# FFN of a hybrid diffusion layer: up-projection by one level of Strassen's algorithm, down-projection as a token-major stage of its own

## The reference

```python
D_MODEL = 1024; SEQ = 128; DEC_SEQ = 1024; D_FF = 2816
def rmsnorm(x, gain):
    y = xf * lax.rsqrt(jnp.mean(xf * xf, axis=-1, keepdims=True) + EPS)
    return (y * gain).astype(x.dtype)
def conv_ffn(h, w_up, conv_w, conv_b, w_down):
    u = h @ w_up                                  # (tokens, 2 * D_FF)
    up = jnp.pad(u, ((0, 0), (1, 1), (0, 0)))
    u = up[:, :-2] * conv_w[0] + up[:, 1:-1] * conv_w[1] + up[:, 2:] * conv_w[2] + conv_b
    a, b = jnp.split(u, 2, axis=-1)
    return (jax.nn.silu(a) * b) @ w_down
...
    h = rmsnorm(xs, norm2[l]) * (1.0 + sc2) + sh2
    xs = xs + g2 * conv_ffn(h, w_up[l], conv_w[l], conv_b[l], w_down[l])
y_sample = rmsnorm(xs, final_norm)                # and the same for the context tokens
```

## Time and profile before

| | us |
|---|---|
| median of 3 runs | 2656.23 (2655.0 to 2657.93) |
| profiled execution, its span | 2655.1 |
| PE busy in the span | 2551.0 (96%) |
| PEld busy | 2357.2 (89%) |
| DVE busy | 1698.7 (64%) |
| ACT busy | 1031.5 (39%) |
| POOL busy | 837.8 (32%) |

### The profile page before, as it was taken

How to read it: one execution, slowest core, us unless ns; L and a number is a source line. 1 busy time by engine, 2 the same in 40 slices (tenths; PEclk the granted TensorE clock), 3 DMA queues, 4 the chain that set the end, 5 groups by cost and what they waited for, 6 DMA issues and landing times. The chain is left out here.

```text
span 2655.1 us, 40132 instructions
## 1 busy us (share of the span) xinstructions
PE 2551.0 (96%) x14417; PEld 2357.2 (89%) x14417; DVE 1698.7 (64%) x2807; ACT 1031.5 (39%) x1924; POOL 837.8 (32%) x779
## 2 busy tenths in 40 slices
PE   5999999999998999999999999999999999999997
PEld 3899999999997977788778776798999999999997
DVE  5046556646748368787687677456776677766775
ACT  5223323323323256666666667433122221122114
POOL 1122223223223433433433325633222222322322
PEclk9999999999999999999999999999999999999999
DMA  9611111111110200010010012302111111111111
GB/s 320 202 36 49 37 41 42 44 34 50 44 36 27 63 12 9 25 40 9 25 47 9 2 52 70 114 22 64 42 46 39 40 47 39 39 47 39 39 32 72
DMA packets 164537, 135.92 MB, mean 51 GB/s; under 512 B 18492, under 2 KB 142300, under 8 KB 164444
## 3 DMA queue, kind: packets, MB, share of 16 engines
q1 hardware_dynamic: 163228, 129.99, 15.8%
q10 hardware_dynamic: 1216, 4.72, 0.5%
HBM read 120.41 MB, written 14.29 MB: 51 GB/s over the span
## 5 line engine op out<-in xcount | busy, mean ns | idle before, releaser
L390 PE MATMUL mix_ps<-act_hi,w_hi 128*128 128x384 f32 (+1 forms) x1320 | 443.4, 336 | 6.1 <-ACT conv L2494 3.0
L391 PE MATMUL mix_ps<-act_lo,w_hi 128*128 128x384 f32 (+1 forms) x1320 | 442.4, 335 | 0.0
L392 PE MATMUL mix_ps<-act_hi,w_lo 128*128 128x384 f32 (+1 forms) x1320 | 442.2, 335 | 0.0
L390 PE MATMUL proj_ps<-act_hi,w_hi 128*128 128x384 f32 x1152 | 406.9, 353 | 3.3 <-ACTq L743 3.3
L392 PE MATMUL proj_ps<-act_hi,w_lo 128*128 128x384 f32 x1152 | 387.1, 336 | 0.0
L391 PE MATMUL proj_ps<-act_lo,w_hi 128*128 128x384 f32 x1152 | 387.0, 336 | 0.0
L2604 DVE SCALAR_TENSOR_TENSOR resid_t<-mix_ps,mod,resid_t 128x384 f32<-128x384 f32 (+2 forms) x640 | 273.9, 508 | 134.5 <-PE mix_ps L392 134.5
L1946 DVE TENSOR_TENSOR probs_lo<-mix_ps,probs_hi 128x512 fp32r<-128x512 f32 x324 | 222.7, 688 | 142.5 <-ACT mix_ps L1741 138.9
L1740 ACT ACTIVATE probs_hi<-mix_ps 128x512 fp32r<-128x512 f32 x324 | 193.6, 598 | 183.8 <-PE mix_ps L1540 182.2
L390 PEld LDWEIGHTS mix_ps<-act_hi,w_hi 128*128 128x128 f32 x1320 | 248.4, 188 | 11.6 <-issue 5.4
L2582 DVE SCALAR_TENSOR_TENSOR conv<-up,conv_t,conv 128x127 f32<-128x127 f32 (+1 forms) x168 | 211.4, 1317 | 73.2 <-ACT conv L2510 61.5
(11 more groups left out here) (301 smaller groups left out, 5403.5 us busy)
## 6 DMA issues: line engine op xcount, KB each, us to landing
w_raw<-in_w_in SPq DMA_DIRECT2D x64, 512.0 KB, 3.8
w_raw<-in_w_up SPq DMA_DIRECT2D x44, 512.0 KB, 3.8
ada_w<-in_ada_w SPq DMA_DIRECT2D x7, 2048.0 KB, 15.4
w_raw<-in_w_down SPq DMA_DIRECT2D x22, 512.0 KB, 3.5
q_k_dec<-in_ada_w SPq DMA_DIRECT2D x5, 2048.0 KB, 8.0
out<-xy SPq DMA_DIRECT2D x9, 512.0 KB, 2.7
w_raw<-in_w_o SPq DMA_DIRECT2D x8, 512.0 KB, 5.3
xy<-in_x_sample SPq DMA_DIRECT2D x8, 512.0 KB, 6.7
```

Of the source, the lines that this page charges most:

```text
L390: nc.tensor.matmul(out, w_hi, x_hi, start=(k == 0), stop=False)
L391: nc.tensor.matmul(out, w_hi, x_lo, start=False, stop=False)
L392: return nc.tensor.matmul(out, w_lo, x_hi, start=False, stop=last)
```

## The change

- **Up.** For pairs 1 to 21 the product of a pair is one level of Strassen's algorithm (the form with seven products). The 1024 input features are halved (K1, K2), the tokens are taken in two pieces p of 576, each halved again into 288 (Q, the slices N1 and N2), and the two feature blocks of the pair are the two halves of the output. A piece then takes seven products, each over four k-tiles, 12 matmuls of 288 columns, in place of eight block products. Sums of the activations are made once (`token_sums` in place in `resid_t`, high parts by ACT and low parts by DVE); sums of the weights are made for each pair by POOL (`weights`), whose seven operands are split by ACT (high parts) and POOL (low parts), 512 elements a row each. The results are put together by five DVE additions and two ACT copies a piece (`taken`). Convolution, silu and gate run a piece behind, on 575 or 577 tokens.
- **Gated rows through DRAM.** The gated result goes unsplit to `g_dram`.
- **Down.** A stage of its own after the last pair: 66 steps d = 22 g + f, each with one w_down block (all 22 are read three times) and one 384-token slice of gated rows. Tokens are now the stationary operand and 512 output features the moving one: 18 matmuls of 512 columns a step, added up in six PSUM banks over the 22 pairs of a group. The residual, kept as rows in DRAM (`x1_dram`, 18 stores, made by transposes in stage 1 and 2), is added once per token tile (`residual_rows`), then the final norm.
- `final_norm` and the gates are loaded as rows; the transposes at the end are gone. `normed` works in place in `resid_t`, so `normed_hi` has two ACT instructions where there was one. Phase 2 clears 46 semaphores on POOL at its start.

```diff
+    x1_dram = nc.dram_tensor("resid_scratch", (NT, P, D), F32, kind="Internal").ap()
+    g_dram = nc.dram_tensor("gated_scratch", (FB, P, T), F32, kind="Internal").ap()
...
+        Q = T // 4
+        K1, K2 = slice(0, 4), slice(4, 8)
+        N1 = [slice(2 * Q * p, 2 * Q * p + Q) for p in range(2)]
+        N2 = [slice(2 * Q * p + Q, 2 * Q * p + 2 * Q) for p in range(2)]
+        OUT = [(0, 2 * Q - 1), (2 * Q - 1, T)]
+        SLOT_H = [WH[:, 2, K1], WH[:, 2, K2], WX[:, 0], WH[:, 0, K1], WH[:, 0, K2], WH[:, 1, K1], WH[:, 1, K2]]
+        SLOT_L = [WL[:, 2, K1], WL[:, 2, K2], WX[:, 1], WL[:, 0, K1], WL[:, 0, K2], WL[:, 1, K1], WL[:, 1, K2]]
+        W_SUM = [None, 1, 2, 0, None, None, 1]
+        RAW = [W_RAW[:, 0, K1], None, None, None, W_RAW[:, 0, K2], W_RAW[:, 1, K2], None]
+        SRC = [RAW[i] if W_SUM[i] is None else ST[:, W_SUM[i]] for i in range(7)]
...
# SyncE
+                store_g(0, 0, C_G + 1)
+                load_up(2, 1)
+                with sp.Fori(0, FB - 3) as r:
+                    store_g(r, 1, r * 2 + (C_G + 2))
+                    store_g(r + 1, 0, r * 2 + (C_G + 3))
+                    load_up(r + 3, r + 2)
...
+                store_g(FB - 3, 1, 2 * (FB - 3) + C_G + 2)
+                store_g(FB - 2, 0, 2 * (FB - 3) + C_G + 3)
+                sp.wait_ge(w_ok[5], F)
+                load_wd(0)
+                load_wd(1)
+                store_g(FB - 2, 1, 2 * (FB - 2) + C_G + 2)
+                store_g(FB - 1, 0, 2 * (FB - 2) + C_G + 3)
+                for p in range(2):
+                    sp.wait_ge(g_st[p], 16 * F + 1)
+                sp.wait_ge(w_ok[6], F)
+                for d in range(3):
+                    load_g(d)
+                store_g(FB - 1, 1, 2 * (FB - 1) + C_G + 2)
+                sp.wait_ge(prod, C_P + 14 * F)
+                sp.wait_ge(gate_st, 32)
+                for i in range(3):
...
# GpSimd, in place of split(s, f, n)
-                def split(s, f, n):
-                    pool.wait_ge(raw_in[s], f * 16 + 16)
-                    if s < 2:
-                        pool.wait_ge(up_done, f * 6 + (3 * s - 3 + C_UP))
-                    else:
-                        pool.wait_ge(dn_done, f * ND + 1)
-                    pool.sem_inc(w_go, 1)
-                    nc.gpsimd.tensor_copy(WH[:, s], WR[s]).then_inc(w_hi, 1)
-                    pool.wait_ge(w_hi, n)
-                    nc.gpsimd.tensor_tensor(WL[:, s], WR[s], WH[:, s].bitcast(F32), ALU.subtract).then_inc(w_split[s], 1)
+                def weights(f, sums, his, ahead):
+                    for s in range(2):
+                        pool.wait_ge(raw_in[s], ahead)
+                    nc.gpsimd.tensor_tensor(ST[:, 0], W_RAW[:, 1, K1], W_RAW[:, 1, K2], ALU.add).then_inc(w_sum, 1)
+                    nc.gpsimd.tensor_tensor(ST[:, 2], W_RAW[:, 0, K1], W_RAW[:, 1, K1], ALU.subtract).then_inc(w_sum, 1)
+                    pool.wait_ge(w_sum, sums + 1)
+                    nc.gpsimd.tensor_tensor(ST[:, 1], ST[:, 0], W_RAW[:, 0, K1], ALU.subtract).then_inc(w_sum, 1)
+                    low(0, his + 1)
+                    low(1, his + 2)
+                    pool.wait_ge(w_ok[1], f)
+                    nc.gpsimd.tensor_tensor(ST[:, 1], W_RAW[:, 0, K2], ST[:, 1], ALU.subtract).then_inc(w_sum, 1)
+                    for i in range(2, 7):
+                        low(i, his + i + 1)
...
# TensorE, in place of up_part and down_part
-                def up_part(f):
-                    for s in range(2):
-                        pe.wait_ge(w_split[s], f + 2)
-                        for g in range(NG):
-                            n = NG * s + g
-                            pe.wait_ge(up_out, f * 6 + (n - RING_UP + 1 + C_UO))
-                            for k in range(KC):
-                                m = three_pass(nc, up[:, n % RING_UP, 0:G], WH[:, s, k], WL[:, s, k],
-                                               HH[:, k, g * G:(g + 1) * G], HL[:, k, g * G:(g + 1) * G], k, k == KC - 1)
-                            m.then_inc(up_done, 1)
+                def product(p, i, bank, adds):
+                    hi, lo = sums(p, i)
+                    out = ps[:, bank, 0:Q]
+                    for k in range(4):
+                        nc.tensor.matmul(out, SLOT_H[i][:, k], hi[:, k], start=(k == 0 and not adds), stop=False, skip_group_check=adds)
+                        nc.tensor.matmul(out, SLOT_H[i][:, k], lo[:, k], start=False, stop=False, skip_group_check=adds)
+                        m = nc.tensor.matmul(out, SLOT_L[i][:, k], hi[:, k], start=False, stop=(k == 3), skip_group_check=adds)
+                    m.then_inc(prod, 1)
+                    weight(0)
+                    pe.wait_ge(act_ev, 2 * g + 1)
+                    product(p, 0, p, False)
+                    weight(1)
+                    pe.wait_ge(dve_ev, 5 * g + 2)
+                    if first:
+                        pe.wait_ge(sum_lo[p], 2)
+                    product(p, 1, 2, False)
+                    weight(2)
+                    pe.wait_ge(dve_ev, 5 * g + 3)
+                    product(p, 2, 3, False)
+                    weight(3)
+                    pe.wait_ge(dve_ev, 5 * g + 1)
+                    if first:
+                        pe.wait_ge(sum_lo[p], 4)
+                    product(p, 3, 4 + p, False)
+                    weight(4)
+                    pe.wait_ge(act_ev, 2 * g + (C_A + 1))
+                    product(p, 4, p, True)
+                    weight(5)
+                    pe.wait_ge(dve_ev, 5 * g + 5)
+                    product(p, 5, 6, False)
+                    weight(6)
+                    pe.wait_ge(dve_ev, 5 * g + (C_D + 3))
+                    product(p, 6, 4 + p, True)
+                pe.sem_inc(prod, C_P)
...
+                for d in range(ND):
+                    g, f = divmod(d, FB)
+                    pe.wait_ge(wd_ok, d + 1)
+                    pe.wait_ge(gd_ok, d + 1)
+                    for i in range(3):
+                        n = 3 * g + i
+                        if f == 0:
+                            if g == 0:
+                                pe.wait_ge(act_ev, C_A + 4 * F)
+                                pe.wait_ge(dve_ev, C_D + 10 * F - 5 + (0, 2, 4)[i])
+                            elif n == 3:
+                                pe.wait_ge(dve_ev, C_D + 10 * F)
+                            else:
+                                pe.wait_ge(z_out, 2 * (n - 4) + 2)
+                        for half in range(2):
+                            out = ps[:, SETS[n % 4][half], :]
+                            cols = slice(half * 512, half * 512 + 512)
+                            gh, gl = (GHL[:, d % 3, b, i * P:(i + 1) * P] for b in range(2))
+                            nc.tensor.matmul(out, gh, WDH[d % 3][:, cols], start=(f == 0), stop=False)
+                            nc.tensor.matmul(out, gl, WDH[d % 3][:, cols], start=False, stop=False)
+                            m = nc.tensor.matmul(out, gh, WDL[d % 3][:, cols], start=False, stop=(f == F))
+                        if f == F and i < 2:
+                            m.then_inc(tile_done, 1)
+                    m.then_inc(d_done, 1)
...
# VectorE
+                def token_sums(p):
+                    h11, h12, h21, h22 = X1[:, K1, N1[p]], X1[:, K1, N2[p]], X1[:, K2, N1[p]], X1[:, K2, N2[p]]
+                    dve.wait_ge(lo_ok, 16 + 8 * p)
+                    nc.vector.tensor_tensor(h11, h12, h11, ALU.subtract).then_inc(sum_ok[p], 1)
+                    nc.vector.tensor_tensor(h12, h22, h12, ALU.subtract).then_inc(sum_ok[p], 1)
+                    dve.wait_ge(sum_ok[p], 1)
+                    nc.vector.tensor_tensor(h22, h22, h11, ALU.subtract).then_inc(sum_ok[p], 1)
+                    dve.wait_ge(sum_ok[p], 3)
+                    nc.vector.tensor_tensor(h21, h21, h22, ALU.subtract).then_inc(sum_ok[p], 1)
...
+                def taken(r, p):
+                    g = r * 2 + p
+                    before = r if p == 0 else r + 1
+                    base = r * 12 + 8 if p == 0 else r * 12 + 12
+                    conv(1 - p, before, base, g * 2 + 2)
+                    dve.wait_ge(prod, 7 * g + (C_P + 2))
+                    dve.wait_ge(act_ev, 2 * g + (C_A + 1))
+                    nc.vector.tensor_tensor(TMP[:, 2, :], ps[:, 2, 0:Q], TMP[:, p, :], ALU.add).then_inc(dve_ev, 1)
+                    gate(1 - p, r * 12 + (12 if p == 0 else 20), g + 2, before * 16 + 1)
+                    dve.wait_ge(prod, 7 * g + (C_P + 3))
+                    dve.wait_ge(dve_ev, 5 * g + (C_D + 1))
+                    nc.vector.tensor_tensor(TMP[:, 3, :], ps[:, 3, 0:Q], TMP[:, 2, :], ALU.add).then_inc(dve_ev, 1)
+                    dve.wait_ge(prod, 7 * g + (C_P + 4))
+                    dve.wait_ge(dve_ev, 5 * g + (C_D + 2))
+                    nc.vector.tensor_tensor(U[:, 1, N2[p]], ps[:, 4 + p, 0:Q], TMP[:, 3, :], ALU.add).then_inc(dve_ev, 1)
+                    dve.wait_ge(prod, 7 * g + (C_P + 6))
```

(3 more changed lines are left out.)

782 lines of the change are left out of this document (438 added, 344 removed).

## The result

The changed kernel takes 2694.25 us (median of four runs, 2691.8 to 2696.18) against 2657.08 before: a ratio of 1.0138, 95% interval 1.0123 to 1.0152. It is 37 us slower. The forecast was 2638, faster; the range ended at 2675. The profiled execution took 2696.2, its span is 2694.4.

The account below looks back on a forecast made before the run. PE, busy 96%, was taken as the bound. 45.7 + 479.4 + 3.2 + 289 + 12.7, plus 3 for half clock, gave 833 against 857.5; with +5.2 before that stretch, 2638 us, range 2600 to 2675.

Parts of the forecast that it names:

- The price of the port in the loop: Up loop: DVE and POOL exclude each other on the SBUF port, making PE wait 1.0 us a pair; 22.83 a pair.
- so three fit and not four: Second half of a pair: program order lets three POOL instructions of about 1.1 us delay DVE's taps and gate.
- critical half: Second half of a pair, where the larger piece is convolved; PE's seventh product has 2 us slack there.
- The other half of a pair: Up loop: slack 1.5 us more than its own holds, so costed at nothing.
- a hold: Up loop: time a POOL two-input instruction keeps DVE off the shared port, about 1.1 us each.
- the loop's chain misses the clock: Rival for the up loop: a fourth hold or late ACT centre tap makes a pair 25 us, total 2683; chance 0.17.
- From T0 to the first Strassen product: From the end of the last output-projection product: DVE's order with port holds puts the first Strassen product at 45.7 us.
- Down stage: From up to down: 6 us idle at the third step, 275 for 66 steps, 8 at group ends; 289 us.
- the clock's share: Allowance of 3 us for PE at half clock behind the two long idles.
- The weights' rival: Down stage goes at the pace of w_down landings, 5 us instead of 3.5; total 2668; chance 0.15.
- Before T0: Up to the last output-projection product's end: 48 row transposes move into the PE-bound output projection, +5.2 us.
- Tail: End of the kernel: no transposes, only rows' addition, square, root and a store; 12.7 us instead of 15.9.

Follow-up runs that it names:

- e1: Changed kernel with POOL's two-input instructions narrowed to 16 of 512 elements from the second Strassen pair on, leaving work out: 2639.4 us in one run.
- e4: Changed kernel with three order edits in the down stage (third w_down block loaded earlier, row loads spread out, residual additions a step earlier): 2629.72 us.
- e9: Changed kernel with POOL's third weight sum waiting for the first centre tap in the second Strassen pair alone: 2652.45 us.
- e6: Changed kernel with one added wait in every pair: POOL's third weight sum only after ACT's first centre tap of the second half: 2662.06 us.
- e10: e8 with the halves taken in the other order, silu behind the second high part and the gate behind the fourth addition: 2640.73 us.
- e5: The changed kernel itself run once more, nothing edited: 2692.55 us.
- e8: Changed kernel with the seventh product in its own PSUM bank and the three down-stage order edits of e4 together: 2625.70 us.

## Why the prediction was wrong

**The price of the port in the loop** is the step that failed ("so three fit and not four"): a pair was to take 22.83, and takes 24.8 (521.3 us between the gates at 1863.85 and 2385.11, 21 pairs). Mechanism, place and releaser were right, and with POOL's instructions narrow (e1) the wait and the slow matmuls behind it are gone. Three things were off. The four POOL instructions that the forecast named for the critical half (two low parts, a sum, a third low part) all held DVE, three the taps and the fourth the gate, so the wait is 2.04 us (between starts) instead of 1.0: about 22 us over the loop. A matmul of 288 columns takes 0.1329, not 0.130: 10 us of the 65.5 that were to be gained. And the clock fell behind some of the waits: with 22.32 x 21 = 468.8 of PE's own time and 43 of waits, some 14 of the 527.5 us are matmuls at the lower level, for which the sum had 3 in all. The other half of a pair was costed at nothing, and no wait of PE stands there.

The size of a hold was about right: the chain without holds is 7.4 us as forecast (11.33 less 3.89), and a hold 0.97. Here the recorded sum has a slip that helped it: 7.4 and three holds of its own 1.1 are 10.7, not the 10.35 that it went on with; three holds of 0.97 do give 10.35.

What the forecast took for one state of the loop was one of two: e4 and e9 run at 23.03, the changed kernel at 24.8. That 23.03 lies near the 22.83 on record is in part luck: PE's own time is 0.48 us a pair longer than forecast, and the wait 0.61 instead of 1.0. Whether all four holds fall into the critical half goes by where POOL's third weight sum lies against the first tap: e6 moved only that, and its pairs went to 23.42. Which rhythm a kernel without such a wait takes is seen in its first pair, but what decides it there stays open. The rival named "the loop's chain misses the clock" is what happened, with the fourth hold as its cause and 24.8 near its 25, though in one half of a pair and not in both; it had a chance of 0.17.

The Trainium skill (SBUF — State Buffer, "Who interferes with whom") says that whichever starts first has the shared ports for the whole instruction, and that issue order decides who is blocked. The traces agree: in e4 the sum that starts ahead of the tap (2208.87) takes its 1.29 us while the first tap waits for it, and the low part that starts while a tap runs (2214.35) takes 1.79. What follows for a loop, two rhythms from one program, the forecast had not drawn. As to the rate at 288 columns, the formula of the Trainium skill (TensorE: Matmul & The Clock Gate, "Back-to-back issue gap"), N/2.4 + 2.5 ns, gives an estimate of 122.5 ns; e1 shows 132.9, so formula and forecast were both low.

**From T0 to the first Strassen product**: 45.7 forecast, 43.6 to 43.7 measured in every run but e10 (45.5). The working by DVE's order with port holds came within 2.1 us; no run tested its terms one by one.

**Down stage**: 289 plus the clock's share, 302.5 measured. The steps take 4.20 us (starts at 2456.42 and 2460.62), not 4.17. The third step was late by 6.6 and 1.5 for slow matmuls behind, about as said. At the group ends the waits were 3.9 and 4.8 us, as said, but each was followed by 1.3 to 1.5 us at the lower clock: 11.4 instead of 8. What was missed is the eighth step, 5.7 us late: the forecast costed landings by their median of 3.5, and not a block behind a clump of six loads of rows in SP's queue. The weights' rival, a slower pace through all 66 steps, did not occur.

**Before T0**: +10.8 instead of +5.2. The output projection with its 48 more transposes took 6.3 us more (106.1 against 99.8). The rest, 4.5, stood ahead of this stage in the profiled execution (first transpose of rows of x at 1702.3 against 1697.8 in the trace of before), but in those of e4 and e5 that transpose stands at 1696.7 and 1697.7: it is not the change's.

**Tail**: 12.7 forecast, 12.4 measured.

Of the 65.5 us that PE was to save, 55 are real (e1). In the changed kernel the loop alone gives back 59, more than all of it, and the waits of start and down stage come on top. e8, at 2625.7, keeps some 30 of the 55.

## What to carry to other kernels

Where two engines share a port and a third takes turns with both, count not only the holds but where each starts: such a loop can settle in more than one rhythm, and the same program then takes two times 40 us apart. Before an added instruction is given the credit, look in the trace whether the loop had already started otherwise. Ask what a wait is for before pricing it: a PSUM bank that lay unused took 46 us off, while moving POOL's work about gained 20 to 30. Look at every place where a queue issues several loads ahead of one that is due; a median landing time says nothing about that one.

## What the runs showed of the hardware

- An added wait can shorten a program: e6 by 30 us.
- One program's loop ran at 23.03 us a pair (e4) or at 24.46 and 26.0 (the changed kernel), for twenty pairs on end.
- A wait of PE of about 2.4 us at the seventh product was followed by 12 matmuls 0.24 us apart (granted clock 0.50) in the changed kernel; one of 1.17 us at the same place in e4 was not. Of twenty waits of 2.04 us each later in the loop, six were followed by 15 or 16 such matmuls, from 1.0 to 1.5 us after PE had gone on, and fourteen by none.
- PE's starts went by columns only nearly: 0.1329 us at 288 columns, 0.1733 at 384, 0.2333 at 512.
- POOL's two-input instruction of 512 elements took 1.28 us alone and 1.7 to 1.8 when it met DVE; DVE's tap of 447 elements 0.68 alone and 1.24 on average beside it.
